# Low parts written over the loaded weights, and a new map of expert places, in a fused decoder block

## The reference: what is computed

```python
z = rmsnorm(x, mix_norm) @ w_in              # pool, q, k, v, indexer, gates
merged = gates[0] * (pool_mixer(z_pool) @ w_branch_pool) \
       + gates[1] * (dsa_attention(q, k, v, qi, ki, wi) @ w_branch_attn)
x = x + merged @ w_out
h2 = rmsnorm(x, ffn_norm)
logits = h2 @ w_router + b_router            # top 4 of 32, softmax over the four
for e in range(32):                          # every expert's weights are needed
    gu = h2 @ w1[e] + b1[e]                  # 1024 x 2048
    out += combine[:, e:e+1] * (swiglu(gu) @ w2[e] + b2[e])   # 1024 x 1024
return rmsnorm(x + out, final_norm)
```

## Time and profile before

| | |
|---|---|
| median of 3 runs | 1103.54 us (1103.14 to 1104.28) |
| profiled execution, its own time | 1103.12 us |
| its span | 1101.2 us |
| PE busy | 1021.2 us (93%) |
| DVE, ACT, POOL busy | 303.5 (28%), 218.6 (20%), 18.3 us (2%) |
| DMA, mean | 398 GB/s, 438.34 MB |

### The profile page before, as it was taken

One profiled execution on the slowest core, in us unless ns is written; L12 is line 12 of the kernel. 1 busy time (PEld: TensorE's weight loads), 2 busy tenths in 40 slices (PEclk: granted clock), 3 DMA queues, 4 the chain that ended last, 5 costly groups with the idle time before them and its releaser, 6 DMA issues.

```text
span 1101.2 us, 12231 instructions
## 1 busy us (share of the span) xinstructions
PE 1021.2 (93%) x4994; PEld 503.4 (46%) x4994; DVE 303.5 (28%) x689; ACT 218.6 (20%) x373; POOL 18.3 (2%) x26
## 2 busy tenths in 40 slices
PE   5999999999999999998998989898989898999896
PEld 5987776434343434343434343434333343434342
DVE  5866576221212121212121211212121111121212
ACT  6456644111111111111111101011101111111112
POOL 1100020000000000000000000000000000000000
PEclk9999999999999999999999999999999999999999
DMA  8784469999999999999999999999999999999994
GB/s 321 290 329 148 153 258 417 426 430 430 431 431 428 436 432 430 437 430 432 432 438 431 432 432 438 431 432 432 438 431 432 432 438 431 432 427 430 432 428 183
DMA packets 25635, 438.34 MB, mean 398 GB/s; under 512 B 3016, under 2 KB 3200, under 8 KB 5120
## 3 DMA queue, kind: packets, MB, share of 16 engines
q1 hardware_dynamic: 24432, 432.84, 92.5%
q0 software_dynamic: 1168, 5.01, 1.2%
HBM read 436.78 MB, written 2.11 MB: 399 GB/s over the span
## 4 chain that ended last, share of the span: by engine, by line
PE 67%; DMA 27%; DVE 2%; issue 1%; ACT 1%; SPq 0%; DVEq 0%; ACTq 0%
PE bank L1424 28%; DMA quad<-in_w 21%; PE bank L1473 14%; DMA place<-in_w 6%; PE bank L1085 6%; PE bank L1086 5%; PE bank L1087 5%; PE bank L1329 3%; PE bank L1286 1%; PE bank L1454 1%; DMA cst<-in_consts 1%; PE bank L1397 1%; PE bank L1379 1%; PE bank L1433 0%; DVE wl L712 0%
## 5 line engine op out<-in xcount | busy, mean ns | idle before, releaser
L1424 PE MATMUL bank<-quad,r 128*64 128x512 f32 x1280 | 294.4, 618 | 22.2 <-DMA quad<-in_w 22.2
L1424 PEld LDWEIGHTS bank<-quad,r 128*64 128x64 f32 x1280 | 98.3, 142 | 205.9 <-issue 201.5
L1424 PE MATMUL bank<-place,r 128*64 128x512 f32 x704 | 154.6, 595 | 4.8 <-DMA place<-in_w 3.7
L1473 PE MATMUL bank<-quad,r 128*64 128x512 f32 x640 | 141.7, 595 | 11.2 <-issue 7.8
L996 DVE TENSOR_SCALAR r<-bank 128x512 f32<-128x512 f32 x32 | 22.1, 692 | 404.9 <-PE bank L1424 391.9
L1018 DVE TENSOR_TENSOR ysl<-bank,ysh 64x512 fp32r<-64x512 f32 x62 | 42.7, 688 | 291.1 <-ACT ysh L662 290.1
L643 ACT ACTIVATE r<-r 128x512 f32<-128x512 f32 x32 | 20.2, 632 | 471.0 <-DVE r L996 471.0
L1424 PEld LDWEIGHTS bank<-place,r 128*64 128x64 f32 x704 | 49.4, 137 | 102.4 <-issue 94.9
L1473 PEld LDWEIGHTS bank<-quad,r 128*64 128x64 f32 x640 | 51.1, 137 | 90.5 <-issue 90.5
L1473 PE MATMUL bank<-place,r 128*64 128x512 f32 x352 | 78.0, 595 | 6.0 <-issue 5.3
L662 ACT ACTIVATE ysh<-bank 64x512 fp32r<-64x512 f32 x62 | 36.6, 591 | 225.6 <-PE bank L1473 224.8
(11 more groups left out here) (214 smaller groups left out, 815.4 us busy)
## 6 DMA issues: line engine op xcount, KB each, us to landing
quad<-in_w SPq DMA_DIRECT2D x60, 4096.0 KB, 29.3
place<-in_w SPq DMA_DIRECT2D x69, 2048.0 KB, 17.7
ring<-in_w_front SPq DMA_DIRECT2D x24, 1024.0 KB, 4.9
place<-in_w SPq DMA_DIRECT2D x2, 1024.0 KB, 34.7
place<-in_w_last SPq DMA_DIRECT2D x1, 2048.0 KB, 36.0
place<-in_w_last SPq DMA_DIRECT2D x2, 1024.0 KB, 34.7
ring<-in_w_idx SPq DMA_DIRECT2D x2, 768.0 KB, 6.8
xs<-in_x SPq DMA_DIRECT2D x2, 512.0 KB, 8.2
```

The lines of the kernel that those rows point to most:

```text
L1424: ins = mm(bk[part, :], xgT[i // 2 % 2][:, k, own], w[:, c1:c1 + HALF], start=False, stop=k == KD - 1)
L1473: ins = mm(YT[part, :], a_k, w[:, kk, c1:c1 + HALF], start=k == 0, stop=k == KD - 1)
```

## The change

The low part of a piece is written where the piece was loaded: a float32r view of the ring slot (`ring_low`) takes the place of the four `wl` buffers. A slot is free only when PE has used its pieces, so the load of use u waits for `piece_used` instead of `low_ready`. The 4096 floats saved become a third expert place that nothing in the front uses (`o_early` is three chunks wide); in exchange the ring's slots and the four `wh` buffers together with the bias tile fill three places, where bias and ring filled two and the split buffers two. The number of places stays ten. The order of the first chunks: chunks 0, 1, 2 after uses 11, 13, 15; chunk 3 (masks) ahead of use 23; chunk 4 (gates) behind the merge and ahead of use 25; chunks 5 to 8 after pieces 48, 50, 52, 52; chunk 9 as before. The order in which the places of chunks 40 to 47 are filled changes with the map. The load of b1 moves on POOL from behind the merge and piece 44 to ahead of the merge, behind piece 40.

```diff
-        o_ring = top[0]
-        ring = new("ring", FRING * SLOT).rearrange("p (r n) -> p r n", r=FRING)
+        o_slots = {2: top[0], 0: top[0] + SLOT, 1: top[0] + SLOT + CHUNK}
+        o_wh = [o_slots[i // 2] + SLOT + i % 2 * PIECE for i in range(LOOK)]
+        ring = [at(f"ring{i}", o_slots[i], SLOT) for i in range(FRING)]
+        ring_low = [at(f"ring_low{i}", o_slots[i], SLOT, f32r) for i in range(FRING)]
+        wh = [at(f"wh{i}", o_wh[i], PIECE, f32r) for i in range(LOOK)]
+        top[0] += SLOT + 2 * CHUNK
         o_early = top[0]
-        top[0] += 2 * CHUNK
+        top[0] += EARLY * CHUNK
...
-        o_split = top[0]
-        wh, wl = [], []
-        for i in range(0, LOOK, 2):
-            for tiles, name in ((wh, "wh"), (wl, "wl")):
-                tiles += [new(f"{name}{i + j}", PIECE, f32r) for j in range(2)]
...
-        first = [o_early, o_early + CHUNK, o_masks, o_gates, o_bias, o_bias + CHUNK, o_split, o_split + CHUNK, o_hT, o_xs]
+        first = [o_early, o_early + CHUNK, o_early + 2 * CHUNK, o_masks, o_gates, o_bias, o_bias + CHUNK, o_bias + 2 * CHUNK,
+                 o_hT, o_xs]
...
-        order = [c % PLACES for c in range(END - 2 * QUADS)] + [0, 1, 4, 5, 3, 6, 7, 8]
+        order = [c % PLACES for c in range(END - 2 * QUADS)] + [1, 2, 5, 6, 7, 0, 4, 8]
...
                 if use >= FRING:
-                    sp.wait_ge(low_ready, 2 * (use - FRING) + 2)
-                sp.dma_start(ring[:, use % FRING, 0:n], src).then_inc(ring_loaded[use % FRING], 16)
+                    sp.wait_ge(piece_used, 2 * (use - FRING) + 2)
+                sp.dma_start(ring[use % FRING][:, 0:n], src).then_inc(ring_loaded[use % FRING], 16)
...
-                if use == 24:
+                if use == 23:
                     sp.wait_ge(hmax_ready, 2 * NH)
                     sp.wait_ge(piece_used, P_BA)
-                    chunk(0, 2, place[2], chunk_loaded[2])
+                    chunk(0, 3, place[3], chunk_loaded[3])
+                elif use == 25:
+                    sp.wait_ge(merged, 4)
+                    chunk(0, 4, place[4], chunk_loaded[4])
                 load(use, w_front[use - 2, :, :], SLOT)
-                if use in (11, 13):
+                if use in (11, 13, 15):
...
             former_use = (
-                ((merged, 4),),
-                ((logit_read, NH), (low_ready, 50)),
-                ((low_ready, 52),),
+                ((logit_read, NH), (piece_used, N_PIECES - 4)),
                 ((piece_used, N_PIECES - 2),),
                 ((piece_used, N_PIECES),),
                 ((piece_used, N_PIECES),),
                 ((gather_done, 1),),
             )
-            for c in range(3, END):
+            for c in range(5, END):
...
+            pool.wait_ge(piece_used, P_BA)
+            pool.dma_start(b1s, b1.rearrange("i p n -> p i n")).then_inc(b1_loaded, 16)
+
             for n, q in enumerate(ORDER):
...
             pool.wait_ge(piece_used, P_WO)
-            pool.dma_start(b1s, b1.rearrange("i p n -> p i n")).then_inc(b1_loaded, 16)
             pool.dma_start(b2s, b2).then_inc(b2_loaded, 16)
...
-                nc.vector.tensor_tensor(piece_cols(wl[n % LOOK], n), ring_piece(n),
+                nc.vector.tensor_tensor(low_piece(n), ring_piece(n),
                                         piece_cols(wh[n % LOOK], n).bitcast(f32), ALU.subtract)\
```

More of the change, by code:

```diff
@@ L55 @@
 FRING = 3
+EARLY = 3
 PIECE = SLOT // 2
@@ L288, in hybrid_block @@
         END = FIRST * GROUP * CHUNKS
-        first = [o_early, o_early + CHUNK, o_masks, o_gates, o_bias, o_bias + CHUNK, o_split, o_split + CHUNK, o_hT, o_xs]
-        assert len(first) == PLACES and o_masks + SLOT == o3 and o_xs + SLOT == o1 and o_early == o_bias + 2 * CHUNK
+        first = [o_early, o_early + CHUNK, o_early + 2 * CHUNK, o_masks, o_gates, o_bias, o_bias + CHUNK, o_bias + 2 * CHUNK,
+                 o_hT, o_xs]
+        assert len(first) == PLACES and o_masks + SLOT == o3 and o_xs + SLOT == o1 and o_early == o_bias + 3 * CHUNK
         place = [at(f"place{i}", off, CHUNK) for i, off in enumerate(first)]
         quad = [at(f"quad{i}", o_bias + 2 * i * CHUNK, 2 * CHUNK) for i in range(QUADS)]
-        order = [c % PLACES for c in range(END - 2 * QUADS)] + [0, 1, 4, 5, 3, 6, 7, 8]
+        order = [c % PLACES for c in range(END - 2 * QUADS)] + [1, 2, 5, 6, 7, 0, 4, 8]
         plan = []
@@ L311, in piece_cols, with slot_piece, low_piece @@
             return t[:, 0:2 * N_IDX if n < P_Q else PIECE].rearrange("p (k n) -> p k n", k=2)
+        def slot_piece(tiles, n):
+            o = (n % 2) * (2 * N_IDX if n < P_Q else PIECE)
+            return piece_cols(tiles[(n // 2) % FRING][:, o:], n)
         def ring_piece(n):
-            o = (n % 2) * (2 * N_IDX if n < P_Q else PIECE)
-            return piece_cols(ring[:, (n // 2) % FRING, o:], n)
+            return slot_piece(ring, n)
+        def low_piece(n):
+            return slot_piece(ring_low, n)
         @block.sync
@@ L357, in _ @@
             )
-            for c in range(3, END):
+            for c in range(5, END):
                 if c < PLACES:
-                    for signal, n in former_use[c - 3]:
+                    for signal, n in former_use[c - 5]:
                         sp.wait_ge(signal, n)
@@ L1089, in piece_idx @@
             def piece_idx(n):
-                h, l = piece_cols(wh[n % LOOK], n), piece_cols(wl[n % LOOK], n)
+                h, l = piece_cols(wh[n % LOOK], n), low_piece(n)
                 for i in range(2):
@@ L1126, in piece_product @@
                 k = n - n0
-                h, l = wh[n % LOOK], wl[n % LOOK]
+                h, l = wh[n % LOOK], low_piece(n).rearrange("p k n -> p (k n)")
                 for i, q in enumerate(order):
@@ L1146, in attention_branch @@
                             pe.wait_ge(low_ready, n + 1)
-                        h, l = wh[n % LOOK][:, c * HALF:(c + 1) * HALF], wl[n % LOOK][:, c * HALF:(c + 1) * HALF]
+                        h, l = wh[n % LOOK][:, c * HALF:(c + 1) * HALF], low_piece(n)[:, c, :]
                         for b in range(TB):
```

## The result

| | before | after |
|---|---|---|
| median, this comparison | 1103.34 us (4 runs) | 1111.28 us (4 runs, 1110.80 to 1112.28) |
| ratio, 95% interval | | 1.0074 (1.006 to 1.0089) |
| profiled execution: own time, span | 1103.12, 1101.2 us | 1111.07, 1109.3 us |

What follows compares the result with a forecast made beforehand. It took the kernel as bound by one full DMA stream at 432 GB/s behind a front, with PE fixing the stream's start. Terms -1.5 + 0 + 1.1 + 0.4 + 0 = 0.0 gave 1103.6 us, range 1101.7 to 1107.3.

Steps and rivals of the forecast that it cites:

- The ring waits for PE: Front: ring loads leave only when PE has used the slot's pieces; PE's work hides 7.2 of 10.9 us, cost nothing.
- load 4: Start of the front, pieces 8 and 9: issued at 22.2 as POOL's transfers begin, cost 1.1 us (0 to 4.0).
- My price if the cover were gone: Front, behind early chunks: 1 to 2 us of other ACT or DVE work would cost as much at three places.
- My last sign of being wrong: Front: the prediction is wrong if PE waits for a ring load anywhere after piece 20.
- L = 31.4: Start of the front: assumed landing time of load 4 in us; PE is late by L - 30.35.
- its rival: Start of the front: load 4 late behind POOL's transfers, PE waiting at pieces 9, 16, 17; 1106.4 us, chance 0.27.
- Loads 3 and b1: Load 3 at the start and b1 moved ahead of the merge: both hidden, cost 0.
- The residual adds: End of the front: load 25 lands behind chunk 4, making the adds 0.4 us late (0 to 2).
- The map's gain: Start of the expert stream: lighter by 3.7 us, but chunk 14's issue caps the gain at 1.5 us (0.8 to 2.6).
- every early byte counts: Rival, start of the stream: chunk 14 is no fixed point, 3.7 up to 4.86 us come through; chance 0.12.
- The sum: Whole kernel: -1.5 + 0 + 1.1 + 0.4 + 0 = 0.0 us against the profiled execution, forecast 1103.6 us.

Runs made afterwards that it cites:

- e2: The changed kernel with its three early chunks behind uses 9, 11 and 13 instead of 11, 13 and 15: 1108.85 us.
- e3: The changed kernel with ACT's copies of transposed probabilities and attended values ahead of high(n) for pieces 28 to 43: 1105.74 us, nine runs from 1104.8 to 1111.4.
- e5: The changed kernel with e3's order on ACT, and on DVE the attended low part ahead of low(n): 1104.55 us, ratio to before 1.0009.
- e1: The kernel before with only the wait changed: ring loads wait for piece_used instead of low_ready: 1110.15 us, ratio 1.0065.
- e4: The changed kernel with load 25 issued ahead of chunk 4 and its wait for the merge: 1109.19 us (1106.73 to 1111.07).
- e6: The changed kernel with e5's orders, e2's early chunks and e4's load 25 together: 1103.75 us, ratio to the kernel before 1.0002.
- e10: e6 with the final gain loaded last, when PE has finished w1 of the last expert: 1103.10 us, ratio to the kernel before 0.9998.
- e8: The kernel before without the load of chunk 5 (2 MB, zeros written instead; half of expert 0's w2 product left out): 1102.94 us, ratio 0.9999.

## Why the prediction was wrong

**The step that failed** is "The ring waits for PE": "In the steady front that is 7.2 of 10.9: PE hides it", "Cost nothing". I compared a load's landing with the time when PE needs those weights. That holds in the changed kernel's trace: PE waited for no ring load's own low part. But `high(n)` is an instruction in ACT's order, with the copies behind it that PE needs two pieces sooner than piece n. For `pT` the slack was T(30) less T(29), 3.1 us, less `high(32)`, exponentials and copy, 2.3 us. A load that lands 4.8 us after T(28), 1.0 us behind T(29), uses it up (e2: 0.28 us of wait), and one that lands 7.1 us after T(28) is 2.5 us too late (2.76 measured). I had written the rule down for load 4 ("behind high(8) ACT has the indexer's copies") and didn't apply it to the loads behind it. My price if the cover were gone, "by 1 to 2 us of other work on ACT or DVE, so much at each of three places", was of the right kind, but I left it out of the sum. e3 and e5 show it: two orders on ACT and DVE bring back 6.7 us with every load still waiting for PE. And e1 shows the other side: the changed wait alone costs 7.0 us. My last sign of being wrong was that PE waits for a ring load after piece 20. In the changed kernel it waited there for small results that stood behind ring loads on ACT and DVE.

**What the step cost**: 0 forecast. Measured in the trace, 4.2 us at T(30) to T(32), 0.6 from there to T(40), 2.0 at the branch: 6.8.

**The clock** had no term. The three waits of PE over 2.7 us in the softmax part and at the branch (2.76 us in the changed kernel, 2.97 in e3, 2.92 in e4) were each followed by a stretch at a lower granted clock: 2.76 us of idle went with 4.2 lost in the changed kernel, and 2.97 with 4.8 in e3.

**Load 4 and load 5.** Forecast 1.1 us with L = 31.4 (0 to 4.0), and its rival 0.27 likely. Load 4 landed 4.8 us after its issue at 22.48, at 27.3, so that rival was out. Its issue on SP's timeline and its landing time:

```profile
22.48 0.33 SPq L332 DMA_DIRECT2D ring<-in_w_front  x1
```
```profile
DMA to landing us min/median/max: 4.8/4.8/4.8
```

low(9) started at 34.13, L + 6.8, as forecast. But low(17) started at 61.77, 27.6 us behind low(9) and not 24.3, because DVE stood still ahead of low(10) (timeline of DVE):

```profile
40.08 1.23 DVE L723 TENSOR_TENSOR ring_low<-ring,wh 128x1024 fp32r<-128x1024 f32 x1 [3.42 <-ACT wh L497]
```

That is load 5, which T(6) released only at 32.24 and which landed at 38.9; the sum had no term for it. It was nearly free: PE was 0.5 us late at T(18), and 0.3 of that was there behind piece 1 (17.34, where the earlier trace rows have 17.08), before either load could matter. But it took the slack: in e1, e6 and e10 PE waited 0.9, 0.6 and 1.0 us in all for low(16) and low(17).

The Trainium skill, page "DMA: Bandwidth & Descriptors", section "Queues, rings and completion order", has each DMA engine go round robin between the rings with work. By that rule load 4 would not have had to wait for all of POOL's transfers, and it did not. But no turns are seen in the trace after. The DMA queues in 23.5 to 26.5 us, with SP's load 4 issued 0.3 us ahead of POOL's first large transfer, and in 32.3 to 34.5 us, with load 5 issued behind several of them (packets, MB, share):

```profile
q1 hardware_dynamic: 115, 0.93, 83.6%
q0 software_dynamic: 1, 0.01, 0.6%
```
```profile
q0 software_dynamic: 98, 0.74, 86.7%
```

Each time the queue that was first moved nearly all the bytes. Between 28.5 and 35.5 us of the kernel before, both queues moved bytes, 1.70 MB on SP's and 1.19 on POOL's. What decides between the two cases no run here shows.

**Loads 3 and b1** cost nothing, as forecast.

**The residual adds**: 0.4 forecast, 1.0 measured (T(52) to the gather 12.7 instead of 11.7 us), since load 25 took 9.4 us behind chunk 4, where I had put 8. e4 takes it back.

**The map's gain**: 1.5 forecast (0.8 to 2.6), 0.5 measured, and 0.25 in e8. The mechanism was right, that chunk 14's issue caps it, and so was the rejection of the rival "every early byte counts" (e8, e6). The size was read off chunk landings, 8.6 against 7.1, as if chunk 14 would meet an idle queue. It did not: chunk 13 was in flight. From the landing of chunk 9 to that of chunk 14 it took 26.5 us where it had been 24.5, at 408 GB/s and not 432, and in e8 the same stretch moved 401. Why the stream is slower behind a queue that ran dry stays open.

**The sum** with measured terms: 0.5 (late at T(18)) + 6.8 + 0.3 (last pieces) + 1.0 - 0.5 = 8.1, as in the span.

## What to carry to other kernels

When a wait makes a load later, list what stands behind its first consumer on that engine's program order, and compare with when those results are needed, not with when the data are. In a kernel whose weights form one full stream behind a front, find the first issue in the stream that waits for compute. Here bytes removed ahead of it were worth 0.25 of 4.86 us, a stream made later ahead of it stayed late, and half a megabyte taken out behind it gave about its own time. Where the slack is gone, put the small copies that the bottleneck engine waits for ahead of the large ones that wait for DMA.

## What the runs showed of the hardware

After 2.76 us of idle PE's granted clock was 0.50 for the next 3 us, and 0.99 in the 6 behind them; after 2.92 us in e4 it was 0.51 for 2.6 us. After waits of 1.77 us (e2) and 1.71 (e1) it stayed at 1.00. The ring loads of 1 MB took 4.9 us in the median before, but load 21, with no other load in flight for nearly all of its time, took from 4.8 to 7.1 in the eight traces in which it waits for PE. A chunk on a queue that had run dry took 7.2 us at the first gather of the changed kernel; in e6 it took 9.9.
